# Mixer 0 of a two-layer hybrid decoder trunk: input rows and state parameters on two DMA queues, clearings and both input projection halves placed ahead of the state blocks

## The chip, the cores and the metric

The kernel runs on one core of one Trainium2 chip. The metric is the device time of one execution in microseconds (us), the median of three runs. The engines are named as the profile names them: PE (TensorE, matmul and transpose), DVE (VectorE), ACT (ScalarE), POOL (GpSimd), and SP (SyncE, which only issues DMAs here). A q behind an engine's name (SPq) is its queue of DMA issues.

## What is computed

A trunk of two layers over 256 tokens of width 1024. Each layer adds a token mixer and a channel mixer to the residual stream; only the mixer of layer 0 matters for this change.

```
for l in range(2):
    hn = rmsnorm(x, norm_mix[l])
    x = x + hybrid_mixer(hn, ...)       # mLSTM heads + S5 state-space groups
    hn = rmsnorm(x, norm_ffn[l])
    x = x + (swiglu if l == 0 else moe_swiglu)(hn, ...)
return rmsnorm(x, norm_final)

def hybrid_mixer(h, w_in, ...):
    q, k, v, o, i, f, u = split(h @ w_in)       # u: 512 channels for S5
    ...mLSTM on q, k, v, o with gates i, f...
    # S5, for each of 32 groups g with 64 states p and 16 channels:
    dt = exp(log_dt); ab = exp((a_re + i a_im) * dt)
    bb = (ab - 1) / (a_re + i a_im) * (b_re + i b_im)
    x_t = ab * x_(t-1) + bb @ u_t
    y_t = Re(c @ x_t) + d * u_t
```

## The kernel before, in words

The program is written by hand for each engine: five blocks (SP, POOL, ACT, DVE, PE), each one list of instructions in a fixed order, joined by semaphores. An engine runs its list strictly in order, so an instruction that waits holds everything behind it on that engine.

**Weights.** Weights of 2 MB arrive in a ring of five slots; SP issues their DMAs in the order of `chunk_plan`: u, q, k, v, o of `w_in`, then glu, out and so on. Chunk u (the 512 columns that feed the S5 part) is issued at L802, the other ones at L866, each when the slot's last user has run.

**The start.** SP issues the residual stream x (L800), chunk u (L802), then 17 small DMAs: 12 of parameter rows (L812), 2 of the state matrices' a (L814), log_dt (L816) and 2 gate biases (L818). All 17 count on one semaphore, `s_par`. Then `layer_params(0)` issues b_re and b_im (L823, `b_raw`) and c_re and c_im (L826, `c_raw`), and the gate columns `w_if` (L834). PE's first instruction (L2136) turns the rows into columns (`vec`), and waits for all 17. DVE takes the norm of x (L1296 to L1307), then copies `vec` and `s5p` (L1590 to L1595). PE transposes the normed x (L1956), DVE and ACT copy it out as `hnT` (L1315, L1037).

**The state blocks.** DVE's `prep_factors` (L1323 to L1361, some 38 small operations) works out the discretised factors. `prep_blocks` (L1363 to L1386) clears `blocks` (L1367), multiplies b by the factors into it (L1371 to L1378), copies c into `c_dup` (L1383) and clears `cT` (L1386). PE transposes 4 blocks of b (16 transposes, L1923) and 2 of c (8, L1931); ACT copies b's out (L1025) and DVE c's (`prep_c`, L1396). `turned_c` (L1406 to L1411) makes the c matrices of the even steps and gives `c_ready`, for which only PE's `y` products wait.

**The mixer's order.** On PE (`mixer`, function `channels` at L1969): half 0 of u, the 24 transposes, the gate projection `if` (L2027), the state inputs `bu` of couples 0 and 1 (L1993), half 1 of u, the kernel within a couple `k0` (L1943), and then eight steps, the first of which are: qk 0, bu 2; qk 1, bu 3; y 0 (L2010), qk 2, bu 4; qk 3, bu 5; y 1, v 0, bu 6. A qk is 32 matmuls at L1969. On DVE: `turned_c`, and then for each of eight couples of state pairs one scan block (`s5_couple`, L1422 to L1442, from here on a couple); behind couple 1 the copies of the gates (`gate_start`, L1485 to L1489), behind couple 2 the running sums of the gates (`gate_sums`, L1496 to L1503) and the convolutions (L1472, L1474). On ACT: a copy of each projection (L1085 for u, L1111 for qk), each followed by the sines of one couple (`trig_pair`, L1048 to L1066); behind qk 1 the exp and log of the gates (L1130, L1131), for which `gate_sums` waits. On POOL: the phases of each couple (L957 to L967), and once the decays (L974).

**Banks.** `products()` lists all products in PE's order with the engine that drains each and its PSUM bank; a product waits until the one before it in its bank is drained. The functions `lo` and `hi` hand out banks 0 to 3 and 4 to 7 in turn.

**After the mixer** come the dense SwiGLU, mixer 1 (in the same order, without the state blocks, which `prep_blocks(1)` makes at the end of mixer 0), and the routed SwiGLU, whose weights stream through `m_ring`. Every weight DMA of these stages is released by a product or a copy of the stages before it.

## Time and profile before

| | |
|---|---|
| Median of 3 runs | 1480.25 us (1479.22 to 1481.89) |
| The profiled execution's own time | 1480.46 us |
| Its span in the profile | 1478.4 us |
| PE busy | 1346.0 us (91%) |
| DVE busy | 467.6 us (32%) |
| ACT busy | 278.6 us (19%) |
| POOL busy | 98.0 us (7%) |
| DMA | 423.50 MB, mean 286 GB/s |

The profile is of one execution. Its span runs from the first to the last event of the core; 2.06 us of the execution lie around it. Times in the rows count from the span's start. A timeline merges neighbouring instructions of one line and shape; in its brackets stands how long the engine was idle before, and what ended that wait. Matmul times overlap at their ends, so the distance from one start to the next is what an instruction takes of PE.

### The profile page before, as it was taken

To read this page: it belongs to the slowest core of one execution; us is meant where nothing else is said; L and a number is where in the kernel's file an instruction comes from. 1 tells how busy PE (TensorE), PEld (TensorE's weight loads), DVE (VectorE), ACT (ScalarE), POOL (GpSimd) and SP (SyncE) were. 2 spreads that over 40 slices of the span, in tenths; PEclk is the share of its full clock that TensorE was granted. 3 is DMA by queue.
4 is the path that set the end of the run, shared out by engine and by line. 5 is a ranking of instruction groups with operands and counts; after the bars stand their busy time and mean duration, and the time that the engine had idled before them with its cause. 6 is when DMAs were issued, how large, how long until landed. Compare 5 with 4: busy or idle time off the path is not lost.

```text
span 1478.4 us, 18652 instructions
## 1 busy us (share of the span) xinstructions
PE 1346.0 (91%) x7760; PEld 761.4 (52%) x7760; DVE 467.6 (32%) x1049; ACT 278.6 (19%) x511; POOL 98.0 (7%) x115
## 2 busy tenths in 40 slices
PE   3998879999798886999999999999999999987775
PEld 2765469999785544545445444444433343332321
DVE  6787785555559734022010010101011110100002
ACT  2272234444236200000010100101101001100001
POOL 4240000000343000000000000000000000000000
PEclk9999989999999997999999999999999999999999
DMA  9243055544421208789999959898999999999994
GB/s 283 78 132 132 36 186 207 178 163 150 172 79 65 100 30 354 257 344 409 413 413 411 414 210 418 336 411 337 416 410 412 413 410 414 412 411 416 410 413 203
DMA packets 126734, 423.50 MB, mean 286 GB/s; under 512 B 21632, under 2 KB 23864, under 8 KB 118456
## 3 DMA queue, kind: packets, MB, share of 16 engines
q1 hardware_dynamic: 126648, 422.27, 73.4%
q8 instruction: 64, 1.05, 0.3%
q14 instruction: 22, 0.18, 0.0%
HBM read 421.20 MB, written 1.05 MB: 286 GB/s over the span
## 4 chain that ended last, share of the span: by engine, by line
PE 71%; DMA 14%; DVE 9%; ACT 2%; SPq 2%; issue 2%; POOL 0%; DVEq 0%; ACTq 0%
PE psall L2251 13%; DMA m_ring<-in_moe_w_down_dram 12%; PE psall L2342 11%; PE psall L2265 7%; PE psall L2280 6%; PE psall L1969 3%; PE psall L2353 3%; PE psall L2182 3%; PE psall L2184 3%; PE psall L2183 3%; PE psall L2129 2%; PE psall L2062 2%; PE psall L2228 2%; PE psall L2315 2%; PE psall L2381 2%
## 5 line engine op out<-in xcount | busy, mean ns | idle before, releaser
L2265 PE MATMUL psall<-m_ring,xeT 128*64 128x448 f32 x1024 | 204.2, 547 | 23.0 <-DMA m_ring<-in_moe_w_up_dram 23.0
L2342 PE MATMUL psall<-m_ring,hidT 128*64 128x512 f32 (+1 forms) x672 | 201.0, 597 | 16.0 <-DMA m_ring<-in_moe_w_down_dram 15.1
L2251 PE MATMUL psall<-m_ring,xeT 128*128 128x448 f32 x512 | 195.7, 543 | 0.8 <-DVE xeT L1834 0.8
L2265 PEld LDWEIGHTS psall<-m_ring,xeT 128*64 128x64 f32 x1024 | 74.0, 137 | 141.1 <-issue 139.9
L2251 PEld LDWEIGHTS psall<-m_ring,xeT 128*128 128x128 f32 x512 | 97.3, 191 | 94.1 <-issue 92.9
L2342 PEld LDWEIGHTS psall<-m_ring,hidT 128*64 128x64 f32 (+1 forms) x672 | 72.8, 154 | 135.0 <-issue 119.3
L1856 DVE TENSOR_TENSOR hid<-e_silu,psall 64x448 f32<-64x448 f32 x32 | 19.9, 623 | 354.7 <-ACT e_silu L1216 352.8
L2280 PE MATMUL psall<-m_ring,xeT 128*32 128x448 f32 x1024 | 102.0, 542 | 0.0
L1559 DVE TENSOR_TENSOR w_lo<-ring,w_hi 128x1024 fp32r<-128x1024 f32 x66 | 80.5, 1225 | 68.0 <-ACT w_hi L1171 68.0
L2182 PE MATMUL psall<-hnT_hi,w_hi 128*128 128x256 f32 x352 | 99.6, 283 | 1.2 <-DVE hnT_lo L1692 1.2
L2184 PE MATMUL psall<-hnT_hi,w_lo 128*128 128x256 f32 x352 | 99.5, 283 | 0.0
L2183 PE MATMUL psall<-hnT_lo,w_hi 128*128 128x256 f32 x352 | 98.9, 281 | 0.0
L1969 PE MATMUL psall<-hnT,ring 128*128 128x256 f32 x384 | 85.7, 382 | 2.4 <-ACT hnT L1037 2.4
L950 POOL TENSOR_TENSOR small<-small,neg_half 128x1 f32<-128x1 f32 (+2 forms) x14 | 13.6, 974 | 1084.3 <-DVE small L1298 970.3
L1852 DVE TENSOR_TENSOR hid<-e_silu,psall 128x448 f32<-128x448 f32 x16 | 9.9, 622 | 227.3 <-PE psall L2251 226.3
L1171 ACT ACTIVATE w_hi<-ring 128x1024 fp32r<-128x1024 f32 x66 | 69.3, 1060 | 63.5 <-PE psall L2184 35.9
L1969 PEld LDWEIGHTS psall<-hnT,ring 128*128 128x128 f32 x384 | 72.1, 190 | 13.7 <-issue 3.5
L1230 ACT ACTIVATE hidT<-psall 128x224 f32<-128x224 f32 (+5 forms) x48 | 22.3, 481 | 265.4 <-PE psall L2315 265.2
L2182 PEld LDWEIGHTS psall<-hnT_hi,w_hi 128*128 128x128 f32 x352 | 66.6, 189 | 2.1 <-issue 1.4
L2183 PEld LDWEIGHTS psall<-hnT_lo,w_hi 128*128 128x128 f32 x352 | 66.6, 189 | 0.8
L2184 PEld LDWEIGHTS psall<-hnT_hi,w_lo 128*128 128x128 f32 x352 | 66.3, 188 | 0.0
L2280 PEld LDWEIGHTS psall<-m_ring,xeT 128*32 128x32 f32 x1024 | 30.4, 109 | 63.6 <-issue 63.0
(326 smaller groups left out, 1475.2 us busy)
## 6 DMA issues: line engine op xcount, KB each, us to landing
m_ring<-in_moe_w_gate_dram SPq DMA_DIRECT2D x128, 896.0 KB, 20.0
m_ring<-in_moe_w_up_dram SPq DMA_DIRECT2D x128, 896.0 KB, 17.1
m_ring<-in_moe_w_down_dram SPq DMA_DIRECT2D x64, 1792.0 KB, 19.0
ring<-in_w_in_dram SPq DMA_DIRECT2D x10, 2048.0 KB, 12.9
ring<-in_ffn_w_gate_dram SPq DMA_DIRECT2D x5, 2048.0 KB, 10.4
ring<-in_ffn_w_up_dram SPq DMA_DIRECT2D x5, 2048.0 KB, 7.8
ring<-in_ffn_w_down_dram SPq DMA_DIRECT2D x5, 2048.0 KB, 7.9
ring<-in_w_out_dram SPq DMA_DIRECT2D x4, 2048.0 KB, 8.3
```

The source lines that it names most:

```text
L1171: nc.scalar.activation(ffn_split(n, w_hi), ffn_raw(n), ACT.Copy).then_inc(ffn_hi, 1)
L1559: V.tensor_tensor(ffn_split(n, w_lo), ffn_raw(n), ffn_split(n, w_hi).bitcast(F32), ALU.subtract).then_inc(ffn_lo, 1)
L1969: ins = M(bank(name)[:, i * SEQ:(i + 1) * SEQ], w[:, k, a:a + P], hnT[:, k, :], start=(k == 0), stop=(k == KT - 1))
L2062: ins = M(bank(n)[:, :], hnT[:, k, n[2] * P:(n[2] + 1) * P], v3(chunk((n[0], l)), KT)[:, k, :], start=(k == 0), stop=(k == KT - 1))
L2182: M(y, hi[:, k, :], hnT_hi[:, k, :], start=(k == 0), stop=False)
L2183: M(y, hi[:, k, :], hnT_lo[:, k, :], start=False, stop=False)
L2184: ins = M(y, lo[:, k, :], hnT_hi[:, k, :], start=False, stop=(k == KT - 1))
L2251: ins = M(m_bank(key)[:, 0:MH], x[:, i, 0:P], weights(kind, i, s), start=(i == 0), stop=(i == KT - 1))
L2265: ins = M(m_bank(key)[64 * n:64 * n + 64, 0:MH], x[:, i, 0:64], weights(kind, i, s), start=(i == 0), stop=(i == KT - 1))
L2280: ins = M(m_bank(key)[q:q + 32, 0:MH], x[:, i, base:base + 32], weights(kind, i, s), start=(i == 0), stop=(i == KT - 1))
L2342: ins = M(y, hidT[:, r, 0:shape[0]], rows(r, 512 * n, 512), **ends)
L2353: ins = M(ps[7][32 * q:32 * q + 32, cols:cols + 256], hidT[:, r, base:base + 32], rows(r, 256 * q, 256), **ends)
```

## The change

It does five things.

1. On SP, the 17 small DMAs are issued ahead of chunk u. The four DMAs of b and c of layer 0 go to ACT's queue, as the first instructions of ACT (`state_params(act, 0)`); those of layer 1 stay on SP.
2. The clearings of `blocks` and `cT` are a function of their own, `prep_zeros`. For layer 0 it is the first thing that DVE does; for layer 1 it stands right ahead of `prep_blocks(1)`.
3. In mixer 0, PE runs both halves of u and then `if` ahead of the transposes of the state blocks. ACT copies half 1 of u before the b blocks.
4. In mixer 0, DVE runs `turned_c` behind couple 1 instead of ahead of couple 0.
5. The banks of the front are written out. Behind it, some products of both layers get another bank of 4 to 7: the first head products (`mu` of heads 0 and 1) of mixer 0 now stand behind o 0 and y 2 in their banks, where they stood behind y 3 and o 1.

```diff
--- before.py
+++ after.py
@@ -391,15 +391,21 @@
 
     for l in range(DEPTH):
         norm(l, 0)
-        hi(("u", l, 0), "A")
+        out.append((("u", l, 0), "A", 4))
         if l == 0:
-            prep(0)
-        hi(("if", l), "I")
+            out.append((("u", l, 1), "A", 5))
+        out.append((("if", l), "I", 7))
+        if l == 0:
+            for n in B_BLOCKS:
+                lo((n, l), "A")
+            out.append((("c_re", l), "V", 4))
+            out.append((("c_im", l), "V", 5))
         bu(l, 0)
         bu(l, 1)
-        hi(("u", l, 1), "A")
         if l == 0:
-            hi(("k0", l), "A")
+            out.append((("k0", l), "A", 6))
+        else:
+            out.append((("u", l, 1), "A", 5))
         for q, steps in enumerate(mixer_steps(l)):
             for n in steps:
                 if n[0] == "y":
@@ -792,14 +798,19 @@
         def v3(ap, k):
             return ap.rearrange("p (k n) -> p k n", k=k)
 
+        def state_params(eng, l):
+
+            for i, b in enumerate((s5_b_re, s5_b_im)):
+                eng.dma_start(b_raw[:, i, :, :], b[l].rearrange("(g h) s c -> (h s) g c", h=2)).then_inc(s_bc, 16)
+            for i, c in enumerate((s5_c_re, s5_c_im)):
+                eng.dma_start(c_raw[:, i, :, :], c[l].rearrange("(k g) c s -> (g c) k s", k=CT)).then_inc(s_bc, 16)
+
         block = ctx.enter_context(nc.Block())
 
 
         @block.sync
         def _(sp):
             sp.dma_start(x_res[:, :, :], x.rearrange("b (t p) d -> p (b t) d", p=P)).then_inc(s_x, 16)
-            u_cols = w_in[0, :, U0:U0 + DS5].rearrange("(k p) n -> p k n", p=P)
-            sp.dma_start(v3(ring[:, 0, :], KT), u_cols).then_inc(ring_full[0], 16)
             rows = {"norm_mix": norm_mix, "norm_mlstm": norm_mlstm, "s5_d": s5_d, "norm_s5": norm_s5,
                     "norm_ffn": norm_ffn}
             for l in range(DEPTH):
@@ -818,14 +829,12 @@
                 sp.dma_start(b_if[:, :, i], b.rearrange("l h -> h l"),
                              allow_slow_non_contiguous=True).then_inc(s_par, 16)
 
+            u_cols = w_in[0, :, U0:U0 + DS5].rearrange("(k p) n -> p k n", p=P)
+            sp.dma_start(v3(ring[:, 0, :], KT), u_cols).then_inc(ring_full[0], 16)
+
             def layer_params(l):
-                for i, b in enumerate((s5_b_re, s5_b_im)):
-                    sp.dma_start(b_raw[:, i, :, :],
-                                 b[l].rearrange("(g h) s c -> (h s) g c", h=2)).then_inc(s_bc, 16)
-                for i, c in enumerate((s5_c_re, s5_c_im)):
-                    sp.dma_start(c_raw[:, i, :, :],
-                                 c[l].rearrange("(k g) c s -> (g c) k s", k=CT)).then_inc(s_bc, 16)
                 if l:
+                    state_params(sp, l)
                     wait_drained(sp, ("if", l - 1))
                 else:
                     sp.wait_ge(w_if_zero, 1)
@@ -1093,9 +1102,11 @@
                 trig_pair(l, 0)
                 channels_out(l, 0)
                 if l == 0:
+                    channels_out(l, 1)
                     prep_blocks(0)
                 trig_pair(l, 1)
-                channels_out(l, 1)
+                if l:
+                    channels_out(l, 1)
                 if l == 0:
                     prep_k0(0)
                 for q, steps in enumerate(mixer_steps(l)):
@@ -1170,6 +1181,7 @@
                         act.wait_ge(ffn_used, sum(c[0] != "fu" for c in f_parts[:n - SPLIT + 1]))
                 nc.scalar.activation(ffn_split(n, w_hi), ffn_raw(n), ACT.Copy).then_inc(ffn_hi, 1)
 
+            state_params(act, 0)
             for l in range(DEPTH):
                 if l:
                     turns(l, 0)
@@ -1360,11 +1372,15 @@
                 link(V.tensor_tensor(F(16), F(13), F(17), ALU.mult))
                 link(V.tensor_tensor(F(16), F(11), F(16), ALU.add))
 
+            def prep_zeros(l):
+
+                V.memset(blocks[l], 0.0)
+                link(V.memset(cT[:, 0:2, :, :], 0.0))
+
             def prep_blocks(l):
 
                 F = lambda i: fac[:, i, :]
                 dve.wait_ge(s_bc, 64 * (l + 1))
-                V.memset(blocks[l], 0.0)
                 for s, (a, b) in enumerate(((19, 16), (17, 18))):
                     f_re = F(a).unsqueeze(2).to_broadcast([P, PAIRS, GP])
                     f_im = F(b).unsqueeze(2).to_broadcast([P, PAIRS, GP])
@@ -1383,7 +1399,6 @@
                     ins = V.tensor_copy(c_dup[:, :, :, g, :].rearrange("p a b c -> p (a b) c"),
                                         c_raw[:, :, :, :].rearrange("p a b c -> p (a b) c"))
                 ins.then_inc(blk_ready, 1)
-                link(V.memset(cT[:, 0:2, :, :], 0.0))
 
             def prep_c(l):
                 for i, n in enumerate(("c_re", "c_im")):
@@ -1582,6 +1597,7 @@
                                        in1=xs, op0=ALU.mult, op1=ALU.add).then_inc(drained["V"], 1)
 
 
+            prep_zeros(0)
             dve.wait_ge(s_x, 16)
             for t in range(NT):
                 norm_sum(t, hn[:, t, :])
@@ -1603,10 +1619,13 @@
                     prep_factors(0)
                     prep_blocks(0)
                     prep_c(0)
-                turned_c(l)
+                if l:
+                    turned_c(l)
                 for q in range(COUPLES):
                     s5_couple(l, q)
                     if q == 1:
+                        if l == 0:
+                            turned_c(l)
                         gate_start(l)
                     if q == 2:
                         gate_sums(l)
@@ -1670,6 +1689,7 @@
                 out_s5(l, 1, 0)
                 out_s5(l, 1, 1)
                 if l == 0:
+                    prep_zeros(1)
                     prep_blocks(1)
                 for t in range(NT):
                     for c in range(2):
@@ -1979,7 +1999,7 @@
 
                 channel_pair(0)
                 if l == 0:
-                    prep(0)
+                    channel_pair(1)
 
                 def bu(q):
                     c = q // CPC
@@ -2027,13 +2047,16 @@
                     ins = M(bank(n)[0:F_ROW + NH, 0:SEQ], w_if[:, k, :], hnT[:, k, :],
                             start=(k == 0), stop=(k == KT - 1))
                 done(ins)
+                if l == 0:
+                    prep(0)
                 wait_drained(pe, ("u", l, 0))
                 wait_drained(pe, ("b1_im", l))
                 bu(0)
                 bu(1)
-                channel_pair(1)
                 if l == 0:
                     within(0)
+                else:
+                    channel_pair(1)
                 for q, steps in enumerate(mixer_steps(l)):
                     if q + 2 == 2 * CPC:
                         wait_drained(pe, ("u", l, 1))
```

On PE, from its first transposes to the first qk product. Before (L1956: transposes of the normed x; L1969: u and qk; L1923 and L1931: the state blocks; L2027: `if`; L1943: `k0`):

```order
L1956 MATMUL psall<-ident,hn 128x128 x16
L1969 MATMUL psall<-hnT,ring 128x256 x16
L1923 MATMUL psall<-ident,arena 128x128 x16
L1931 MATMUL psall<-ident,arena 128x128 x8
L2027 MATMUL psall<-hnT,w_if 36x256 x8
L1993 MATMUL psall<-arena 128x128 x2
L1993 MATMUL psall<-arena,bT 128x128 x2
```

And in the changed kernel:

```order
L1976 MATMUL psall<-ident,hn 128x128 x16
L1989 MATMUL psall<-hnT,ring 128x256 x32
L2047 MATMUL psall<-hnT,w_if 36x256 x8
L1943 MATMUL psall<-ident,arena 128x128 x16
L1951 MATMUL psall<-ident,arena 128x128 x8
L2013 MATMUL psall<-arena 128x128 x2
L2013 MATMUL psall<-arena,bT 128x128 x2
```

The second half of u and `if` now stand between the first half and the 24 transposes; nothing of the projections is left between the state inputs and `k0`. (One row of matmuls of the program is two on PE: 16 rows of L1969 are 32 matmuls in the trace.)

On DVE, from the copies of c to the gates. Before (L1386: clearing of `cT`; L1396: `prep_c`; L1406 to L1411: `turned_c`; L1422: a couple's first instruction):

```order
L1383 COPY arena<-c_raw 128x8x64 x2
L1386 MEMSET cT 128x1024
L1396 TENSOR_SCALAR cT<-psall 64x16x16 x4
L1406 TENSOR_TENSOR cT<-cT,fac 128x512
L1407 TENSOR_TENSOR arena<-cT,fac 128x512
L1408 TENSOR_TENSOR arena<-cT,fac 128x512
L1409 TENSOR_TENSOR arena<-cT,fac 128x512
L1410 TENSOR_TENSOR cT<-cT,arena 128x512
L1411 TENSOR_TENSOR arena<-arena 128x512
L1422 TENSOR_TENSOR arena<-psall,arena 128x512
```

In the changed kernel, the same place, and then the end of couple 1:

```order
L1399 COPY arena<-c_raw 128x8x64 x2
L1411 TENSOR_SCALAR cT<-psall 64x16x16 x4
L1437 TENSOR_TENSOR arena<-psall,arena 128x512
L1438 TENSOR_TENSOR arena<-psall,arena 128x512
...
L1457 TENSOR_TENSOR hn<-arena 128x256
L1421 TENSOR_TENSOR cT<-cT,fac 128x512
L1422 TENSOR_TENSOR arena<-cT,fac 128x512
L1423 TENSOR_TENSOR arena<-cT,fac 128x512
L1424 TENSOR_TENSOR arena<-cT,fac 128x512
L1425 TENSOR_TENSOR cT<-cT,arena 128x512
L1426 TENSOR_TENSOR arena<-arena 128x512
L1500 COPY arena<-psall 4x256
```

The couples start right behind `prep_c` (L1411), and the six operations of `turned_c` stand between couple 1 and the copies of the gates.

On ACT, the start of the changed kernel, where before the table load stood first:

```order
L804 DMA b_raw<-in_s_b_re_dram 128x16x16
L804 DMA b_raw<-in_s_b_im_dram 128x16x16
L806 DMA c_raw<-in_s_c_re_dram 128x4x64
L806 DMA c_raw<-in_s_c_im_dram 128x4x64
L1046 ACT_TABLE_LOAD
```

ACT issues the four DMAs before its first table load; on SP their four issues are gone from between the gate biases and `w_if`.

## Rows read from the trace of the kernel before

**Rows 1.** Timeline of PE: start us, us, engine line op, count, [idle before <-releaser].
```profile
14.39 0.43 PE L2136 MATMUL psall<-ident,arena 120*128 120x120 f32 x1 [14.39 <-DMA b_if<-in_b_fgate_dram]
...
15.29 3.65 PE L1956 MATMUL psall<-ident,hn 128*128 128x128 f32 x16 [0.31 <-DVE vec L1593]
20.07 7.14 PE L1969 MATMUL psall<-hnT,ring 128*128 128x256 f32 x32 [1.13 <-ACT hnT L1037]
39.43 3.68 PE L1923 MATMUL psall<-ident,arena 128*128 128x128 f32 x16 [12.21 <-DVE arena L1378]
...
44.04 3.64 PE L2027 MATMUL psall<-hnT,w_if 128*36 128x256 f32 x16
...
49.26 7.17 PE L1969 MATMUL psall<-hnT,ring 128*128 128x256 f32 x32
...
57.22 7.14 PE L1969 MATMUL psall<-hnT,ring 128*128 128x256 f32 x32
...
65.38 7.17 PE L1969 MATMUL psall<-hnT,ring 128*128 128x256 f32 x32
```

**Rows 2.** Windows: stretch, us, busy PE, PEld, DVE, ACT, POOL, PEclk, DMA share, GB/s.
```profile
30.00:32.00 2.00, 0.00 (x0) 0.00 (x0) 2.00 (x2) 1.56 (x5) 1.93 (x2) 0.50 1.06 389
...
700.00:1478.00 778.00, 725.22 (x4218) 312.25 (x4210) 72.20 (x133) 72.19 (x144) 1.96 (x2) 0.99 0.96 386
```

**Rows 3.** Timeline of DVE, from the norm of x to couple 1.
```profile
8.95 1.58 DVE L1307 TENSOR_SCALAR hn<-x_res,small 128x1024 f32<-128x1024 f32 x2 [0.25 <-POOL small L950]
...
27.76 1.76 DVE L1367 MEMSET arena<- 128x2048 f32 x1 [0.49 <-DVE fac L1361]
...
43.78 1.75 DVE L1396 TENSOR_SCALAR cT<-psall 64x256 f32<-64x256 f32 x4 [2.54 <-PE psall L1931]
45.56 0.69 DVE L1406 TENSOR_TENSOR cT<-cT,fac 128x512 f32<-128x512 f32 x1
...
50.55 0.69 DVE L1422 TENSOR_TENSOR arena<-psall,arena 128x512 f32<-128x512 f32 x1
...
55.99 0.69 DVE L1422 TENSOR_TENSOR arena<-psall,arena 128x512 f32<-128x512 f32 x1
```

**Rows 4.** Timeline of ACT: the copy of qk 1, and the gates' table load.
```profile
72.59 0.60 ACT L1111 ACTIVATE arena<-psall 128x512 f32<-128x512 f32 x1 [4.83 <-PE psall L1969]
...
75.98 1.28 ACT L1130 ACT_TABLE_LOAD   x1
```

**Rows 5.** Timeline of DVE, from the end of the gates' copies to the heads.
```profile
62.66 0.41 DVE L1489 SCALAR_TENSOR_TENSOR arena<-arena 4x256 f32<-4x256 f32 x1
67.79 0.69 DVE L1422 TENSOR_TENSOR arena<-psall,arena 128x512 f32<-128x512 f32 x1 [4.72 <-ACT arena L1066]
...
73.57 0.42 DVE L1442 TENSOR_TENSOR hn<-arena 128x256 f32<-128x256 f32 x1
79.45 0.41 DVE L1496 SCALAR_TENSOR_TENSOR arena<-arena 4x256 f32<-4x256 f32 x1 [5.46 <-ACT arena L1131]
...
134.44 0.48 DVE L1515 SCALAR_TENSOR_TENSOR arena<-psall,small,cmask 128x256 f32<-128x256 f32 x1 [0.45 <-PE psall L2072]
```

**Rows 6.** Timeline of SP's queue: start and length of each issue.
```profile
1.28 0.46 SPq L802 DMA_DIRECT2D ring<-in_w_in_dram  x1
...
7.94 0.30 SPq L818 DMA_DIRECT2D b_if<-in_b_fgate_dram  x1
```

**Rows 7.** DMA issues of 0 to 16 us: KB each, median us from issue to landing.
```profile
ring<-in_w_in_dram SPq DMA_DIRECT2D x1, 2048.0 KB, 10.2
x_res<-in_x_dram SPq DMA_DIRECT2D x1, 1024.0 KB, 5.1
...
c_raw<-in_s_c_im_dram SPq DMA_DIRECT2D x1, 128.0 KB, 2.6
```

**Rows 8.** Tile b_raw in 60 to 200 us: layer 1's two loads, issue to landing.
```profile
DMA to landing us min/median/max: 4.0/4.2/4.5
```

**Rows 9.** Timeline of PE: 4 transposes of layer 1's blocks.
```profile
187.73 0.63 PE L1923 MATMUL psall<-ident,arena 128*128 128x128 f32 x4
```

## The prediction

> **What bounds the kernel now.** I read the windows first. From 700 us to the end the DMA engines are 96% busy at 386 GB/s and PE 93% [rows 2]: the routed weights stream there. Every weight DMA of that stage is released by an event of the stages before it, so the stage keeps its length and starts when mixer 1 lets it. I take what the front gains to reach the end one for one.
>
> The timeline of PE then shows the front. PE's first instruction waits until 14.39 us for the last small row, its transposes of x start at 15.29, and the first half of u at 20.07. Then it stands still for 12.21 us until DVE has made the state blocks at 39.43, though the second half of u (49.26) and `if` (44.04), which need nothing of DVE, stand behind the blocks [rows 1]. In the hole the granted clock falls to 0.50 [rows 2], 1.2 of 2.4 GHz.
>
> The reader should also see who pays for the late second half. DVE has its first couple at 50.55 [rows 3], but waits 4.72 us ahead of couple 2 and 5.46 us ahead of `gate_sums` at 79.45, both for ACT [rows 5], and ACT had waited 4.83 us for PE's qk 1 [rows 4]. So PE's place in its list sets DVE's `gate_sums`. From there to the heads DVE has hardly a gap; the gain is thus counted at `gate_sums`.
>
> **The change, part by part, on the clock of the profiled execution.**
>
> *Projections ahead of the blocks.* Without any earlier start, PE runs two halves of u (7.14 each) from 20.07 to 34.35, and `if` (3.6, from 44.04 to about 47.6) to 37.9 [rows 1]. DVE's blocks, before at 39.43, lose the clearing of 1.76 us [rows 3] and are there at 37.7. PE and the blocks meet; the hole of 12.21 us is gone. With no hole PE stays at the full clock. The 24 transposes took 4.61 at the half clock (39.43 to 44.04 [rows 1]); four of layer 1's took 0.63 [rows 9], so 24 take 3.8, to 41.7. I take this, and 4.6 as the other bound. `prep_c` (43.78 to 45.56, 1.8 [rows 3]) then ends at 43.5, and the couples can start, since `turned_c` no longer stands ahead of them.
>
> *The clearings.* Both lie on DVE ahead of x, where it is idle (its norm ends at 10.53 [rows 3], it has nothing before x lands, 5.1 us after its issue [rows 7]). They need some 2.7 us (1.76, and half of it for half as many elements); if DVE were late there, up to 2 us would come back. The clearing of `cT` was free before too: it lay inside DVE's wait of 2.54 us for PE [rows 3]. In layer 1 they only change places on DVE: 0.
>
> *DVE's way to `gate_sums`.* A couple took 5.44 (50.55 to 55.99 [rows 3]) with POOL idle for most of it, and 6.2 (67.79 to 73.99 [rows 5]) beside POOL's phases. Now phases lie beside nearly every couple; for couples 0 and 1 I take 5.8 each: 43.5 to 55.1. `turned_c` takes 5.0 (45.56 to 50.55 [rows 3]): 60.1. The gates' copies 1.7 (from couple 1's end, 55.99 + 5.44 = 61.4, to 63.1 [rows 3, 5]): 61.8. Couple 2, 6.2: 68.0.
>
> *PE's and ACT's way to `gate_sums`.* PE does `bu` 0 and 1 (1.7) and `k0` (0.8, up to 57.22 [rows 1]) by 44.3, where `k0` waits for `prep_c`. A qk with its `bu` is 8.16 (57.22 to 65.38 [rows 1]): qk 0 by 52.5, qk 1 by 59.6. ACT needs 3.4 to copy and make the sines (72.59 to 75.98 [rows 4]) and 3.5 for exp and log (to 79.45 [rows 5]): 66.5.
>
> So `gate_sums` stands at 68.0 by DVE and 66.5 by ACT, before at 79.45: **11.4 to 12.9 earlier**. I take 11.8, near the DVE end. The new wait, that y 0 needs `turned_c` (60.1), costs nothing: PE comes to y 0 only behind qk 1 and `bu` 3, at 60.7. Behind y 0 PE has qk 2, which nobody on DVE wants before its second convolution.
>
> *Rows ahead of chunk u.* The last row is issued at 7.94 [rows 6] and lands at 14.39 [rows 1], 6.4 us later, since 3 MB of x and u lie ahead of it in SP's queue; behind no such load a small DMA lands in 2.6 [rows 7]. Now only x is ahead: issued at about 7.5, landed at about 10.3. Then the norm of x becomes the last to come: it ends at 10.53 [rows 3]. The gain has 14.3 less 10.5, or 3.8, as its upper end. The lower end is 0, as b and c now go out beside x. In layer 1 a load of b took 4.0 to 4.5 to land [rows 8], 2 more than a small one, all in short packets. If a share of this falls on x, the norm ends at 11.6. I take **2.6**, nearer to the upper end, because the 3 MB become 1 MB.
>
> The Trainium skill speaks against this part ("DMA: Bandwidth & Descriptors", section "Issuing engines are not separate DMA queues"): DMAs of all issuing engines run on the same 16 DMA engines and interleave, and a second issuer only saves issue time. By that rule the second queue gains nothing for the rows; the b and c packets are mixed with x's, and the sum would move from 1465.6 toward rival B's. No row of before shows two queues at once, so I can't say yet whether the trace agrees.
>
> *Chunk u.* It was issued at 1.28 [rows 6] and landed 10.2 later [rows 7], at 11.5. Now it is issued at about 7.9. By the same 10.2 it lands at 18.1; x (5.1) took half of that, so 13 to 18.1. It is wanted at 20.07 less 2.6, 17.5. I charge nothing; the bound is 0.6, more if b and c hold it up. The chunks q to o follow it; 2 MB at 389 GB/s [rows 2] are 5.4 us, so q is there by 24 and o by 40, and qk 0 begins at 41. ACT's four issues lie ahead of 17 us, where it had nothing to do.
>
> *Banks.* The head's first product no longer waits for y 3's drain: DVE's wait of 0.45 at 134.44 [rows 5] goes. I take **0.4**.
>
> **The sum:** 11.8 + 2.6 + 0.4 = 14.8 us of 1480.46, or **1465.6 us**. The profiled execution lies 0.2 above the median, which I leave aside.
>
> **The rivals.** A measurement can tell 0.2% (3 us) here.
>
> *A. As above.* Bounds: 10.4 (old price of the transposes, DVE's upper durations) to 12.9 for the first part, 0.5 to 3.8 for the second, 0 to 0.9 for the banks. Likely ends: 17.6 and 11, so 1462.9 to 1469.5. Chance 0.70.
>
> *B. The short packets go first.* ACT's b loads (two of 4.0 to 4.5 us [rows 8]) start with x on the same engines and hold it or the rows for all of 3.8 us. For: nothing orders the two queues. Against: their bytes are a quarter of x's. Then only 11.8 + 0.4 is gained: 1468.3. By the skill's rule on interleaving, named above, this case has its ground. Chance 0.13.
>
> *C. Chunk u comes late.* It is the last of 18 issues now, and b and c push it. If it lands at 22, 4.5 after it is wanted, PE and all behind it lose that: 14.8 less 4.5, 1470.2. For: 18.1 by its old landing is already late by 0.6. Against: once it runs, its 2 MB need 5.4 us. Chance 0.10.
>
> *D. The gain does not arrive.* Should the stream of routed weights be paced by something that the front does not move, the time stays at 1480. Against: all its DMAs wait for products of the core. Chance 0.04.
>
> *E. Slower: rows held behind ACT's descriptors.* If SP's 17 issues were each held up, as ACT's b and c are generated at the same time, `s_par` comes late, and with it everything. Each us of it costs one us; it decides from 14.8 us on: rows complete later than at 14.4 + 12.2 = 26.6, instead of 10.3. That takes 17 issues of 1.3 us instead of the 0.38 each that they take now (1.74 to 8.24 on SP [rows 6]). At 30 us the time is 1484. For: a large load on a full queue does block its issuer. Against: rows are few and short. Chance 0.03.
>
> **How the numbers follow.** The forecast is A's, 1465.6. The range 1462.5 to 1470 holds nearly all of A, B, and about half of C: 0.84 of the cases; it is cut no closer, as A's ends are bounds of single terms and not sharp. Faster by over 0.2% are A, B, C: 0.93. Within 0.2%: D, 0.04. Slower: E, 0.03.
>
> **What would show it.** In the new profile: rows complete by 10 to 12 us, transposes of x from 12.7 instead of 15.29; PE busy without a hole from u's first half to the blocks and granted clock 1.0 from 26 to 44 us; the first couple's start near 41; `gate_sums` near 65 instead of 79.45; everything from there, the routed stream too, some 14 us earlier at equal length. Wrong would be: a wait for the ring's DMA ahead of the first half of u (C); x's norm later than 12 (B); a wait ahead of y 0 for `turned_c`; a routed stage that starts earlier and ends at the same time (D).

## The result, and the profile after

| | runs | median, us | range | ratio to before, 95% |
|---|---|---|---|---|
| before, beside the first | 4 | 1480.74 | 1479.22 to 1481.89 | |
| the change | 4 | 1472.62 | 1470.17 to 1473.38 | 0.9943 [0.9926, 0.9960] |
| before, in a later session | 9 | 1480.10 | 1478.81 to 1482.52 | |
| the change again (e13) | 5 | 1469.21 | 1468.99 to 1471.05 | 0.9930 [0.9916, 0.9943] |

The change gains 8.1 us, against 14.8 forecast, and 1472.62 lies outside the range of 1462.5 to 1470. Repeated in another session it gains 10.9, and 1469.21 lies just inside. The profiled execution, the longest of the first four, took 1473.38 us, with a span of 1471.3, 7.1 under that of before. PE is busy for 1351.3 us (92%), DVE for 469.5, ACT for 277.3; DMA still moves 423.50 MB.

The timeline of PE after the change, read against [rows 1] (columns as there):

```profile
11.04 0.43 PE L2159 MATMUL psall<-ident,arena 120*128 120x120 f32 x1 [11.04 <-DMA b_if<-in_b_fgate_dram]
...
11.94 3.65 PE L1976 MATMUL psall<-ident,hn 128*128 128x128 f32 x16 [0.31 <-DVE vec L1609]
16.72 14.05 PE L1989 MATMUL psall<-hnT,ring 128*128 128x256 f32 x64 [1.13 <-ACT hnT L1046]
30.70 3.64 PE L2047 MATMUL psall<-hnT,w_if 128*36 128x256 f32 x16
34.27 1.97 PE L1943 MATMUL psall<-ident,arena 128*128 128x128 f32 x16
...
39.57 7.17 PE L1989 MATMUL psall<-hnT,ring 128*128 128x256 f32 x32
...
78.08 0.65 PE L2030 MATMUL psall<-arena 32*32 32x128 f32 x8 [3.67 <-DVE hn L1457]
...
80.52 8.82 PE L2085 MATMUL psall<-ring,hnT 128*128 128x512 f32 x16
```

The rows arrive 3.35 us earlier (11.04, before 14.39), both halves of u run in one piece from 16.72, and the blocks start at 34.27 instead of 39.43 with no hole ahead of them. But there is a new hole: 3.67 us ahead of y 1, on DVE, and behind it v 0 takes 8.82 us. In the kernel before PE stood 0.88 us there, and v 0 took 7.13:

```profile
92.27 0.42 PE L2010 MATMUL psall<-arena 32*32 32x128 f32 x8 [0.88 <-DVE hn L1442]
...
93.63 7.13 PE L2062 MATMUL psall<-ring,hnT 128*128 128x512 f32 x16
```

DVE's timeline, read against [rows 3, 5]:

```profile
9.15 1.58 DVE L1319 TENSOR_SCALAR hn<-x_res,small 128x1024 f32<-128x1024 f32 x2 [0.25 <-POOL small L959]
...
36.72 1.75 DVE L1411 TENSOR_SCALAR cT<-psall 64x256 f32<-64x256 f32 x4 [1.93 <-PE psall L1951]
...
38.49 0.69 DVE L1437 TENSOR_TENSOR arena<-psall,arena 128x512 f32<-128x512 f32 x1
...
64.25 0.41 DVE L1511 SCALAR_TENSOR_TENSOR arena<-arena 4x256 f32<-4x256 f32 x1
...
96.29 0.43 DVE L1476 SCALAR_TENSOR_TENSOR arena<-arena 128x256 f32<-128x256 f32 x1 [4.22 <-ACT arena L1085]
```

Couple 0 is 12.06 us earlier, and `gate_sums` 15.2 (64.25, before 79.45), a little more than was counted. Then, at 96.29, DVE stands 4.22 us for ACT, where before the same wait was 0.66:

```profile
108.26 0.43 DVE L1461 SCALAR_TENSOR_TENSOR arena<-arena 128x256 f32<-128x256 f32 x1 [0.66 <-ACT arena L1076]
```

In the changed kernel ACT had been waiting itself:

```profile
89.38 0.60 ACT L1127 ACTIVATE arena<-psall 128x512 f32<-128x512 f32 x1 [4.68 <-PE psall L2085]
```

The windows show PE's clock. First the changed kernel: the full front, y 1 and v 0, the first output products, mixer 1's first products, the routed stream (us, busy PE, PEclk, DMA share, GB/s).

```profile
20.00:60.00 40.00, 39.42 (x332) 1.00 0.71 236
78.00:90.00 12.00, 11.92 (x68) 0.75 0.21 81
140.00:154.00 14.00, 12.57 (x40) 0.62 0.00 0
392.00:404.00 12.00, 10.77 (x39) 0.75 0.00 0
700.00:1471.00 771.00, 716.73 (x4170) 0.99 0.96 386
```

The same three middle places in the kernel before:

```profile
92.00:104.00 12.00, 11.73 (x77) 1.00 0.46 170
151.00:165.00 14.00, 12.26 (x45) 0.88 0.01 3
400.00:412.00 12.00, 10.76 (x50) 0.93 0.00 0
```

The front runs at the full clock (PEclk 1.00 is 2.4 GHz, 0.50 is 1.2), as forecast, but in three places behind idle stretches the granted clock is 0.75, 0.62 and 0.75, where it was 1.00, 0.88 and 0.93. The routed stream has its old shape [rows 2].

**Where the 15.2 us went.** The table has the start of the same instruction in profiled executions, as us earlier than in the kernel before. e1 to e15 are the kernels of the next section. hmT are the eight transposes between the output products of mixer 0, and Y 0 is y 0 of mixer 1.

| | before, us | change | e13, again | e1 | e2 | e3 | e4 | e6 | e9 | e11 | e15 |
|---|---|---|---|---|---|---|---|---|---|---|---|
| blocks' transposes | 39.43 | 5.2 | 5.3 | 3.3 | 1.8 | 5.4 | 5.0 | 2.9 | 0.2 | 5.5 | 1.7 |
| `gate_sums` | 79.45 | 15.2 | 15.3 | 3.4 | 11.8 | 15.4 | 15.0 | 12.9 | 0.6 | 15.5 | 11.7 |
| y 2 | 114.26 | 12.0 | 12.5 | 3.4 | 8.7 | 12.5 | 8.1 | 12.3 | 0.6 | 12.8 | 11.0 |
| first output product | 152.05 | 11.1 | 11.8 | 3.4 | 7.8 | 12.1 | 13.8 | 14.6 | 0.9 | 12.9 | 10.2 |
| hmT | 171.50 | 7.8 | 11.4 | 3.4 | 4.5 | 11.8 | 13.8 | 16.4 | 2.7 | 14.7 | 9.7 |
| x transposes, mixer 1 | 397.76 | 9.3 | 11.4 | 3.4 | 6.0 | 11.7 | 13.7 | 18.0 | 2.8 | 14.5 | 9.7 |
| Y 0, mixer 1 | 438.26 | 6.0 | 10.4 | 3.4 | 2.7 | 10.7 | 12.7 | 18.7 | 4.5 | 15.2 | 8.7 |
| routed stage | 581.68 | 7.2 | 11.5 | 3.4 | 3.9 | 8.7 | 13.8 | 22.6 | 7.8 | 18.6 | 9.8 |
| span | 1478.4 | 7.1 | 11.5 | 3.2 | 3.8 | 9.1 | 14.2 | 22.1 | 9.7 | 20.1 | 10.1 |

So the front's gain was whole at `gate_sums` and was lost in steps: 3.2 us by y 2, 0.9 to the output products, 3.3 in the output products, 3.3 at the start of mixer 1; 1.5 came back ahead of the dense SwiGLU and 1.1 behind Y 0 of mixer 1. From the routed stage on nothing changes, as the forecast had it.

### The profile page after: what moved, and what is told of

It is laid out like the page before. It is cut to its first block, busy times and chain, and to the rows that moved or that the text cites. A ratio compares the mean times of both kernels' runs of the same rounds, so it can differ in the third digit from the quotient of the medians.

```text
span 1471.3 us, 18652 instructions
## 1 busy us (share of the span) xinstructions
PE 1351.3 (92%) x7760; PEld 764.5 (52%) x7760; DVE 469.5 (32%) x1049; ACT 277.3 (19%) x511; POOL 96.0 (7%) x115
## 2 busy tenths in 40 slices
DMA packets 126734, 423.50 MB, mean 288 GB/s; under 512 B 21632, under 2 KB 23864, under 8 KB 118456
## 4 chain that ended last, share of the span: by engine, by line
PE 73%; DMA 13%; DVE 9%; ACT 2%; issue 2%; SPq 1%; POOL 0%; DVEq 0%; ACTq 0%
PE psall L2274 13%; DMA m_ring<-in_moe_w_down_dram 12%; PE psall L2365 11%; PE psall L2288 8%; PE psall L2303 6%; PE psall L2376 3%; PE psall L1989 3%; PE psall L2205 3%; PE psall L2207 3%; PE psall L2206 3%; PE psall L2152 3%; PE psall L2085 3%; PE psall L2251 2%; PE psall L2338 2%; PE psall L2404 2%
## 5 line engine op out<-in xcount | busy, mean ns | idle before, releaser
L2365 PE MATMUL psall<-m_ring,hidT 128*64 128x512 f32 (+1 forms) x672 | 201.0, 597 | 17.2 <-DMA m_ring<-in_moe_w_down_dram 16.4
L2152 PE MATMUL psall<-ring,hn 128*128 128x512 f32 x128 | 62.1, 646 | 2.5 <-ACT hn L1169 2.5
## 6 DMA issues: line engine op xcount, KB each, us to landing
m_ring<-in_moe_w_up_dram SPq DMA_DIRECT2D x128, 896.0 KB, 17.1
```

The lines of the kernel that those rows point to most:

```text
L2152: ins = M(bank(n)[:, :], mixT[:, k0 + k, t * P:(t + 1) * P], v3(chunk(("out", l, c)), KT)[:, k0 + k, :], start=(k == 0), stop=(k == 3))
L2365: ins = M(y, hidT[:, r, 0:shape[0]], rows(r, 512 * n, 512), **ends)
```

## The experiments

Two theories. **T1**: the front's gain is real, but PE now runs ahead of DVE; where it then stands, its granted clock falls, and the products behind run at half speed. **T2**: a fixed chain of DVE and ACT absorbs the gain, and the clock is a symptom.

### e1 and e2: the two parts apart

e1 is the kernel before with only the two queues: u's issue moved behind the small rows, b and c of layer 0 on ACT's queue.

```diff
-            sp.dma_start(v3(ring[:, 0, :], KT), u_cols).then_inc(ring_full[0], 16)
...
+            sp.dma_start(v3(ring[:, 0, :], KT), u_cols).then_inc(ring_full[0], 16)
...
+            state_params(act, 0)
```

> The kernel before with part 1 of the change alone (17 rows ahead of chunk u, b and c on ACT's queue). In the changed kernel x's first transposes came 3.35 us earlier (15.29 to 11.94). Theory 1 (what the front gains is real, and PE's granted clock gives part of it back later, by where holes of PE fall): the first transposes are 3.35 earlier, gate_sums near 76.1 instead of 79.45, and the end is 3.35 earlier give or take 2 us by the clock: 1475 to 1479. Theory 2 (from gate_sums on a fixed chain of DVE and ACT absorbs what comes earlier): gate_sums near 76.1, the end within 1 us of before. Theory 3 (the early DMAs disturb later loads): gate_sums later than 76.1.

Measured: 1477.2 us, ratio 0.9981 [0.9971, 0.9991]. The shift of 3.4 stands in every row of the table, to the end.

e2 is the changed kernel without this part, so it has the clearings and the order alone.

> The changed kernel with part 1 undone (chunk u second, then the rows, b and c on SP). Theory 1: gate_sums at 64.25 + 3.35 = 67.6, the hole of PE ahead of y 1 as in the changed kernel (3.7 us), its end some 3 us later than the changed kernel's: 1474 to 1478, with the clock's spread. Theory 2: gate_sums at 67.6 and the end equal to the changed kernel's 1472.6. Sum of the two halves (this one and rows only) against before: theory 1 the same as the whole change's 8.1 within 3 us.

Measured: 1474.28, 0.9953 [0.9939, 0.9966]. 11.8 us at `gate_sums`, 3.8 in the span. The parts add up at `gate_sums` (3.4 + 11.8 = 15.2) and in the profiled spans (3.2 + 3.8 = 7.0, measured 7.1). The part that shifts PE and DVE alike keeps its gain. The part that moves PE against DVE does not: in its profiled execution, the longest of five, two thirds of the 11.8 are lost, by the median, 6.4 us under the kernel before, nearly half. Nothing at the end of the kernel absorbs a gain, which ends rival D.

### e3: idle products in the hole ahead of y 1

The added matmuls, fillers from here on, compute nothing that is used.

```diff
+            def warm(name, n):
+                for _ in range(n):
+                    M(bank(name)[:, 0:SEQ], ident[:, :], cmask[:, :], start=True, stop=True)
...
+                    if (l, c) == (0, 1):
+                        warm(n, 14)
                     pe.wait_ge(tile_done, l * COUPLES + CPC * (c + 1))
```

> The changed kernel; ahead of y 1 in mixer 0, PE fills its hole of 3.67 us with 14 matmuls of 128x256 on constants (some 3.1 us), whose result the product overwrites. Theory 1 (clock): the granted clock stays 1.00 in y 1 and v 0, v 0 takes 7.1 instead of 8.8 and y 1 1.4 instead of 2.4; ACT's copy of v 0 is 2.7 us earlier, DVE's wait ahead of gelu_outer(0) falls from 4.22 to about 1.5, y 2 is 2 to 2.7 us earlier (99.6 to 100.3 instead of 102.28). End 0 to 3 us earlier than the changed kernel. Theory 2 (fixed chain): the same wait of 4.2 and y 2 at 102.3.

Measured: 1471.53, 0.9944 [0.9931, 0.9958]. PE's timeline:

```profile
74.12 6.31 PE L1940 MATMUL psall<-cmask,ident 128*128 128x256 f32 x28
...
81.72 7.13 PE L2091 MATMUL psall<-ring,hnT 128*128 128x512 f32 x16
```

v 0 takes 7.13 us instead of 8.82, but 14 fillers (28 matmuls in the trace) take 6.31, more than the hole, and v 0 starts 1.2 later. The two cancel, so y 2 moves by 0.5 us only. Too large a dose: inconclusive for y 1, done again as e15.

### e4 and e7: useful work in the hole

e4 is the changed kernel with v 0 ahead of y 1 and o 0 ahead of y 2 on PE, in both layers; e7 has the same edit on the kernel before.

```diff
-    return [[("qk", l, 0)], [("qk", l, 1)], [("y", l, 0), ("qk", l, 2)], [("qk", l, 3)], [("y", l, 1), ("v", l, 0)],
-            [("v", l, 1), ("tr", l)], [("y", l, 2), ("o", l, 0)], [("o", l, 1)]]
+    return [[("qk", l, 0)], [("qk", l, 1)], [("y", l, 0), ("qk", l, 2)], [("qk", l, 3)], [("v", l, 0), ("y", l, 1)],
+            [("v", l, 1), ("tr", l)], [("o", l, 0), ("y", l, 2)], [("o", l, 1)]]
```

> The changed kernel with v 0 ahead of y 1 and o 0 ahead of y 2 in both mixers: the holes ahead of y 1 (3.67 us) and y 2 (3.16) are filled with useful products. Theory 1: no hole ahead of y 1, v 0 at the full clock and done near 81.5 instead of 89.3, DVE has no wait ahead of gelu_outer(0) and (1) (4.22 and 2.47 in the changed kernel), and DVE's couples alone set the end of the scans: the last couple ends about 6 us earlier. End 4 to 8 us earlier than the changed kernel in all, both mixers together: 1465 to 1469. Theory 2: DVE's waits go as well, but the tail starts no earlier than y 3, so 1470 to 1473.

> The kernel before, with v 0 ahead of y 1 and o 0 ahead of y 2 on PE, the order that gave 1467.9 on top of the change. It asks whether this order is worth 5 us by itself, or only since the change made PE arrive early. T1: in the kernel before PE stands 0.88 us ahead of y 1, so v 0 delays y 1 by 6 us and with it the outer steps of DVE; gain at y 2 to o 0 at most 3.2 us, loss at y 1; 1477 to 1484. T2 or an order that is better whatever the front does: 1474 to 1476, 5 us less than before.

Measured: e4 1467.91, 0.9921 [0.9906, 0.9936]; e7 1479.52, 1.0000 [0.9989, 1.0011]. On the kernel before the order is worth nothing. On the changed kernel its profiled execution (1466.34, among the two shortest of five) keeps 13.8 us at hmT and 14.2 in the span:

```profile
74.50 7.13 PE L2085 MATMUL psall<-ring,hnT 128*128 128x512 f32 x16
81.56 0.42 PE L2030 MATMUL psall<-arena 32*32 32x128 f32 x8
```

y 1 goes later by 3.5 us and y 2 by 3.8 against the change, yet y 3 comes 4.3 earlier (116.11, changed kernel 120.36): ACT gets v 0 early and does not stand at 89.38 any more. By the trace, then, the changed front wants another order behind it. The times are weaker: e4's interval overlaps that of the repeat (1469.21, [0.9916, 0.9943]), so they alone don't show a gain of the order.

### e9 and e11: the same fillers on both kernels

Both have 6 idle products ahead of head 2's numerator, 3 ahead of head 3's, and 12 ahead of mixer 1's first transposes; e9 on the kernel before, e11 on the changed one.

```diff
+                if (l, what) == (1, 0):
+                    open_bank(pe, ("xT", l, what, 0))
+                    warm(("xT", l, what, 0), 12)
                 pe.wait_ge(hn_ready, (2 * l + what + 1) * NT)
...
                         open_bank(pe, n)
+                        if h >= 2:
+                            warm(n, 6 if h == 2 else 3)
                         wait_drained(pe, ("sc", l, h))
```

> The kernel before with the idle products ahead of head 2 and 3 in both layers and ahead of mixer 1's first transposes, as a control for what the fillers are worth without the change. T1: in the profiled execution of before the clock there was mostly 1.0 already, so little: 1478 to 1480. If the fillers bring 3 us or more here as well, then the half clock behind these holes is a cost of both kernels and not what the change lost.

> The changed kernel with exactly the idle products of e9 (ahead of heads 2 and 3 in both layers, ahead of mixer 1's first transposes), none ahead of y 1 and y 2. Against e9 (1473.4) it prices the change where these three places are at the full clock in both kernels. T1 (the change's gain was lost at the half clock behind idle stretches, in layer 0's y 1 as well as here): about 3 us of the loss (v 0 and y 1) stay, and the rest arrives: 1459 to 1462, a change worth 11 to 14 us. T2 (the loss lies in a chain of DVE and ACT): the change stays worth the 8 us that it was without fillers, 1465.

Measured: e9 1473.40, 0.9954 [0.9942, 0.9966]; e11 1461.83, 0.9885 [0.9869, 0.9901]. T1's 1459 to 1462 for e11 was met, and its 1478 to 1480 for e9 missed: the fillers give 7.4 us in the kernel before too, and 7.4 in the changed one (e13, 1469.21, is of e11's session). So most of the half clock there is a cost of both kernels, not a loss of the change. What it does is spread: with the same program, the output products lost 3.3 us of the shift in the first profile and 0.4 in e13. e11's windows at the output products and at mixer 1's start:

```profile
139.00:153.00 14.00, 14.00 (x55) 1.00 0.00 1
385.00:397.00 12.00, 10.76 (x50) 1.00 0.01 1
```

With the clock held at these places in both, the change is worth 1473.40 less 1461.83, or 11.6 us. Each against the kernel before of its own session makes it 10.9, the two profiled spans 10.4. That leaves 3.6 to 4.8 us of the 15.2, which no clock at these places explains.

### e15: the right dose at y 1

e3 with 8 fillers instead of 14.

> The changed kernel with 8 idle products (3.6 us) ahead of y 1 of layer 0 alone, where PE stands 3.67 us; e3 had 14 there (6.3 us), which delayed y 1 by 2.3 us and so couldn't show what the clock alone costs. T1: y 1 near 78, 1.4 us long, v 0 7.1 us instead of 8.8, y 2 near 99.5 and a shift there of 15 us instead of 12.0 to 12.5; the time 2 to 3 us below 1469 to 1472. T2 (DVE and ACT absorb it): PE at the full clock, y 2 at 101.5 to 102.

Measured: 1470.14, 0.9929 [0.9914, 0.9944].

```profile
77.80 3.72 PE L1940 MATMUL psall<-cmask,ident 128*128 128x256 f32 x16
81.45 0.42 PE L2036 MATMUL psall<-arena 32*32 32x128 f32 x8
...
82.81 7.13 PE L2091 MATMUL psall<-ring,hnT 128*128 128x512 f32 x16
...
103.26 0.65 PE L2036 MATMUL psall<-arena 32*32 32x128 f32 x8 [3.15 <-DVE hn L1457]
```

And DVE's, at the instruction that waited 4.22 us in the changed kernel:

```profile
97.27 0.43 DVE L1476 SCALAR_TENSOR_TENSOR arena<-arena 128x256 f32<-128x256 f32 x1 [0.66 <-ACT arena L1085]
```

Of the numbers expected, y 1 near 78 and y 2 at 99.5 were missed, since this execution's front was 3.5 us slower (`gate_sums` at 67.72, below). Read as a loss between `gate_sums` and y 2, which the front doesn't enter, T1 holds: without fillers the shift falls by 3.2, 2.8, 3.1, 3.0, 2.7 and 3.1 us (the change, e13, e2, e10, e11, e14), with 8 fillers by 0.7 (e15) and 0.6 (e6). So the clock behind this hole costs 2.0 to 2.6 us there. v 0 takes 7.13 us with fillers and 8.4 to 8.8 without, and from 81 to 93 us the granted clock is 1.00. The chain of T2 exists, but it hands on what PE does: ACT copies v 0 (89.38 above) ahead of the sines and of what DVE waits for at 96.29, and with the fillers DVE's wait is 0.66, as in the kernel before. The time expected, 1466 to 1470, was missed by a little, and the time itself doesn't tell e15 from the changed kernel. In the time such fillers show only where the later holes are filled too (e6, below).

### e14: a shared bank in mixer 1

```diff
         else:
-            out.append((("u", l, 1), "A", 5))
+            out.append((("u", l, 1), "A", 4 + (turn["hi"] + 1) % 2))
```

> The changed kernel, with u 1 of layer 1 in PSUM bank 4 instead of 5 and nothing else. In both traces of the changed kernel PE stands 0.78 us ahead of qk 0 of mixer 1, waiting for ACT's copy of u 1 (in the kernel before it ran through), since both products now have bank 5; from u 1's start to Y 0 mixer 1 takes 36.6 us in every changed kernel at the full clock, 35.6 in the kernel before. If the shared bank is the cause: no wait ahead of qk 0, 35.6 us again, and the end 1.0 us earlier, near 1468.3 (a difference that the timing alone can hardly show, the trace can). If not: 36.6 as before.

Measured: 1470.63, 0.9930 [0.9917, 0.9942]. PE in mixer 1, first e13, then e14:

```profile
403.59 7.17 PE L1989 MATMUL psall<-hnT,ring 128*128 128x256 f32 x32
411.54 4.77 PE L1989 MATMUL psall<-hnT,ring 128*128 128x256 f32 x21 [0.78 <-ACT arena L1094]
```

```profile
406.15 14.08 PE L1989 MATMUL psall<-hnT,ring 128*128 128x256 f32 x64
```

The wait is gone, and from u's start to Y 0 mixer 1 takes 35.60 us, as in the kernel before (35.59); e13 took 36.61. The change costs 1.0 us there, by giving u 1 of layer 1 the bank that qk 0 has next. But it does not reach the end. From Y 0 to the routed stage the changed kernel and e13 take 142.2 us, e14 143.4, as the kernel before (143.4): what e14 wins ahead of Y 0 it lacks behind it. Why the stretch behind Y 0 is shorter with the shared bank stays open. Nor does the median show a gain.

### e10: `turned_c` back ahead of couple 0

```diff
-                if l:
-                    turned_c(l)
+                turned_c(l)
                 for q in range(COUPLES):
...
-                        if l == 0:
-                            turned_c(l)
                         gate_start(l)
```

> The changed kernel with one part undone: the turned C blocks of layer 0 are made ahead of couple 0 again and not behind couple 1. My sum counted DVE's 5.0 us of it as only moved (it lies ahead of gate_sums in both places), with couple 0 five us later and y 0 nearer. T1: gate_sums within 0.5 us of the changed kernel's 64.24; PE has to wait for couples 0 to 1, and the time stays within 3 us of 1472.6. Rival (this order is a separate gain): gate_sums and the end 4 to 5 us later, 1477.

Measured: 1471.50, 0.9937 [0.9923, 0.9951]. `gate_sums` stood at 66.14, 1.9 us later, but so did the blocks already (36.15, changed kernel 34.27). Behind the blocks it costs nothing; `turned_c` is only moved, as counted. One small thing is different: PE has no idle time ahead of y 0 here. In the changed kernel `turned_c` ends at 56.38 us, and y 0 starts 0.2 behind it:

```profile
56.59 0.42 PE L2030 MATMUL psall<-arena 32*32 32x128 f32 x8 [0.56 <-issue]
```

### e13: the change once more

> The changed kernel once more, without any edit, for its interval and for a second profiled execution. T1: where the clock falls differs from one execution to the next, so the shift at hmT (7.8 us) and at mixer 1's Y 0 (6.0 us) may differ by 1 to 4 us while that at y 2 (12.0) stays; the shift at gate_sums stays at 15.2. T2: all shifts repeat within 0.5 us.

Measured: 1469.21, 0.9930 [0.9916, 0.9943]. `gate_sums` (15.3) and y 2 (12.5) repeat within 0.5 us; hmT is 11.4 instead of 7.8 and Y 0 10.4 instead of 6.0:

```profile
78.00:90.00 12.00, 12.00 (x73) 0.79 0.21 80
139.00:153.00 14.00, 12.57 (x44) 0.80 0.00 0
390.00:402.00 12.00, 10.76 (x51) 0.99 0.00 0
```

One part of the loss, y 1 and v 0 (0.79, the change 0.75), is there in both. The others, 2.9 of the 3.3 us in the output products and 2.3 of the 3.3 in mixer 1, come and go with the execution.

### e6, e8, e12, e16, e17: toward a better version

e6 is e11 with 8 fillers ahead of y 1 and 6 ahead of y 2 in layer 0; e8 is e4 with e11's. e12 adds to e8 6 fillers ahead of `bu` of couple 3 and 3 ahead of y 2 in layer 0, 8 ahead of the router's transposes and 5 ahead of its positions:

```diff
+                elif (l, what) == (1, 1):
+                    open_bank(pe, ("xT", l, what, 0))
+                    warm(("xT", l, what, 0), 8)
...
+                                    if (l, i) == (0, 6):
+                                        warm(n, 6)
...
+                    if l == 0 and c == 2:
+                        warm(n, 3)
...
+            open_bank(pe, ("pos",))
+            warm(("pos",), 5)
             pe.wait_ge(route_mask, 1)
-            open_bank(pe, ("pos",))
```

e16 is e12 with e14's bank, and e17 is e16 with this:

```diff
+                if l == 0:
+                    open_bank(pe, ("u", l, 0))
+                    warm(("u", l, 0), 3)
                 have_hnT(l, 0)
                 chunk_wait(pe, ("u", l))
```

> The changed kernel with idle products (identity by mask, 256 columns, about 0.45 us each at the full clock) put in front of PE's waits: 8 ahead of y 1 and 6 ahead of y 2 of layer 0 (the idle times there are 3.67 and 3.16 us), 6 ahead of the numerator of head 2 and 3 ahead of head 3's in both layers (2.95 and 1.43 us), 12 ahead of the first transposes of mixer 1 (6.99 us). They compute nothing that is used. Theory T1 (the idle time lowers the granted clock, and the products behind it run at half speed): y 1 takes 1.4 us instead of 2.4, v 0 7.1 instead of 8.8, the shift against the kernel before stays near 12 us at hmT (7.8 without fillers) and near 11 at mixer 1's Y 0 (6.0 without), and the time is 1467 to 1469. Theory T2 (a chain of DVE and ACT absorbs it, the clock is a symptom): PE shows the full clock, but y 2 and hmT stand where they stood, 1471 to 1474.

> The changed kernel with both: v 0 ahead of y 1 and o 0 ahead of y 2, and the idle products ahead of head 2 and 3 and of mixer 1's first transposes. T1: the half clock behind the remaining holes goes, z and the output products and mixer 1's u run at full speed: another 1 to 3 us below the 1467.9 of the order alone, 1465 to 1467. T2: 1468.

> A candidate for the best version: v 0 ahead of y 1 and o 0 ahead of y 2 in both layers, the idle products of e8, and more of them ahead of bu of couple 3 (6) and y 2 (3) in layer 0, ahead of the transposes for the router (8) and ahead of its positions (5). T1: 1 to 3 us below the 1456.3 and 1459.0 of the two earlier versions, 1454 to 1457. If the fillers fill up a place where PE is itself the bound, it is slower than those, 1458 to 1461.

> e12 (1454.4) with u 1 of layer 1 in bank 4. As for e14: 1 us, 1453.4, or nothing.

> e16 with 3 idle products between the transposes of x and u in layer 0, where PE stands 1.1 to 1.8 us. In five profiled executions so far u's 64 products took 14.05 us and the blocks' transposes began at 34.0 to 34.3; in four they took 15.6 to 16.0, with the first 14 of them at half rate, and the blocks' transposes began at 36.2 to 36.5. If that is the clock behind this idle time, the blocks start at 34 to 34.5 here and the median falls by about 1 us, to 1452; if it is something else (chunk u still arriving), u takes 14 to 16 us again.

| | median, us | range | ratio, 95% |
|---|---|---|---|
| e6 | 1456.34 | 1454.62 to 1458.44 | 0.9832 [0.9819, 0.9845] |
| e8 | 1459.01 | 1458.06 to 1460.32 | 0.9857 [0.9843, 0.9872] |
| e12 | 1454.44 | 1451.31 to 1455.95 | 0.9823 [0.9809, 0.9836] |
| e16 | 1453.64 | 1452.82 to 1457.07 | 0.9820 [0.9805, 0.9835] |
| e17 | 1452.16 | 1451.30 to 1453.39 | 0.9807 [0.9795, 0.9820] |

Fillers ahead of y 1 and y 2 of layer 0 are all that e6 has more than e11, and they bring 5.5 us (1461.83 to 1456.34; the intervals of the ratios are apart). The order of e4 in their place (e8) brings 2.8, with intervals that just touch. e6 gained 12 us more than T1 had asked of it, since T1 had priced the half clock by its difference to the kernel before. e17 beats both kernels: 28.4 us under the one before, 17 to 20 under the change. e16's bank can't be told from nothing by the time, nor can e17's fillers from e16.

## Why the prediction was wrong

**What held.** The rows: 3.35 us, counted 2.6. The way to `gate_sums` without them (e2): 11.8, counted 11.8. That it is equal is in part luck. The sum for DVE gave 11.4, and 11.8 was chosen above it; in e2 couple 0 starts at 41.89, 1.6 earlier than the 43.5 counted, and from there to `gate_sums` DVE takes 25.8 us, 1.3 more than counted. The first is the price of the transposes: 24 took 2.9 us (34.27 to 37.13), not 3.8. DVE sets `gate_sums`, and the clock is 1.00 from 20 to 60 us. `turned_c` behind couple 1 costs `gate_sums` nothing (e10), though y 0 does wait for it by some 0.6 us, which the prediction had named as a sign of being wrong; PE has time to spare there, since it stands 3.67 us at y 1. The clearings delay the norm of x by 0.2 us (it ends at 10.73, before 10.53), and the rows come later still (11.04). The stream keeps its length, and whatever reaches it reaches the end (e1). Rivals B and E did not come. The DMA issues of the changed kernel (KB, us to landing):

```profile
x_res<-in_x_dram SPq DMA_DIRECT2D x1, 1024.0 KB, 5.2
b_raw<-in_s_b_re_dram ACTq DMA_DIRECT2D x1, 128.0 KB, 6.7
b_raw<-in_s_b_im_dram ACTq DMA_DIRECT2D x1, 128.0 KB, 7.8
```

x lands 5.2 us after its issue, before 5.1 [rows 7]. b beside it takes 6.7 and 7.8; in the kernel before, behind x and u in SP's queue, the same two loads took 6.0 and 6.8, and layer 1's, later, 4.0 to 4.5 [rows 8]. The Trainium skill says that DMAs of several issuing engines interleave on the same DMA engines ("DMA: Bandwidth & Descriptors", "Issuing engines are not separate DMA queues"). The trace fits that, with b paying and not x. Its further step, that a second issuer saves only issue time, is not refuted by e1's 3.4 us. The rows stood ahead of b and c in SP's queue before too, so the likely cause is that chunk u no longer stands ahead of them; no run has the new order without the second queue.

**The step that failed** is "I take what the front gains to reach the end one for one", with "From there to the heads DVE has hardly a gap". I priced the hole that the change removes and none that it makes. PE gained more than DVE (17.0 us at y 0, 15.2 at `gate_sums`), and the list behind it was written for a late PE. It is ahead of DVE by 3.67 us at y 1, falls to the half clock, and v 0 takes 8.82 us instead of 7.13, at a place where ACT, and through it DVE, now wait for PE. The shift loses 2.7 to 3.2 us between `gate_sums` and y 2 in six kernels without fillers there, and 0.6 to 0.7 in two with them (e15, e6), so 2.0 to 2.6 of it are the clock. By the trace of e4 the order avoids most of it. With the later losses (below), 7.1 and 11.5 of the 15.2 us reach the end in the two profiled executions of the change.

**A second step, of a different kind.** "In layer 1 they only change places" was said of the clearings. I had no term for the projections of layer 1, whose banks the change sets anew: +1.0 us at Y 0 (e14), which comes back behind it. The **banks** term of 0.4 was right at its place and does not last. DVE's wait ahead of the heads is gone, and from y 3 to the first head product PE takes 0.75 us less; by the numerator of head 2 0.2 of that is lost, and 0.7 more in this numerator, which runs at the half clock behind an idle stretch of 2.95 us (with e11's fillers this last loss is 0.03).

**The account**, for the changed kernel as e13 shows it: 15.3 at `gate_sums`, less 2.8 to y 2, less 0.5 in o 0 and o 1 behind y 2's own hole (15.35 us, before 14.80; e6, with fillers there, gains 1.7 instead), plus 0.75 for the banks, less 0.2, less 0.7 in the numerator of head 2. That is 11.8 at the output products. Then 0.4 go in these and 1.0 for the bank of layer 1, and 1.2 come back behind Y 0: 11.5 at the routed stage. These are the rows of one execution, and not a test of the account. Beside it stand 10.9 in the median of e13, and 10.4 to 11.6 for e11 against e9. The first measurement's missing 3 to 4 us lie in the output products and in u of mixer 1, at 0.62 and 0.75 of the clock.

**The range.** Its bounds came from single durations of the front. A term for the clock behind holes that exist in both kernels was missing; in two profiled executions of one program it moves the span by 4.4 us (1471.3 and 1466.9). The sum itself is 1465.7, not 1465.6, which changes nothing.

## What to carry to other kernels

When a front is sped up, follow the engine that gains most to the first place where it is now too early. It stands there, and behind it at the half clock, and what it does then may be what another engine waits for. Look for work that can be put into that place before you count the gain (e4: 13.8 of 15.0 us kept at hmT in its trace, from a change of order that gives 0 without the faster front). And give every fixed buffer that a change assigns a line of its own in the sum, in each layer, then follow it to the end: e14's microsecond is won at Y 0 and gone at the routed stage.

## What was not expected of the hardware

Idle stretches of PE of 2.95 and 1.43 us ahead of heads 2 and 3 of layer 0, the same places of layer 1, and one of 7 us ahead of mixer 1 cost 7.4 us together, in both kernels alike; a few products that compute nothing win them back (e9, e11). The Trainium skill states the mechanism ("TensorE: Matmul & The Clock Gate", Part 1): the clock is halved by default and activity releases it. The trace agrees: in the output products and at mixer 1's start the granted clock is 0.62 and 0.75 in the changed kernel, and 1.00 in both with e11's fillers.

The granted clock of the windows doesn't always tell. In e15 u's 64 products of layer 0 took 17.11 us, in the changed kernel 14.05; the windows name 1.00 for both. First e15's window, then the durations of the 64 products (ns, least, median, most; e15, then the changed kernel):

```profile
17.00:21.00 4.00, 3.88 (x9) 1.00 0.68 166
```

```profile
L1993 PE MATMUL psall<-hnT,ring x64: 379/379/764, 17.1 to 33.9; 128*128 128x256 f32 x64
```

```profile
L1989 PE MATMUL psall<-hnT,ring x64: 378/380/455, 16.7 to 30.4; 128*128 128x256 f32 x64
```

Some of e15's took 764 ns, twice the 379 of the others, and their weight loads up to 337 ns instead of 190. Of 14 profiled executions with both halves of u in a row, nine took 14.05 us, and five (e6, e10, e12, e14, e15) 15.6 to 17.1. With it goes the start of the blocks' transposes, 34.0 to 34.8 or 36.2 to 37.7 (e2, without the earlier rows, left aside), and `gate_sums` by 2 to 3.5 us. PE stands 1.1 to 1.8 us ahead of u in all of them without fillers there. That it is the clock behind this idle time is likely from the 764; e17 with fillers there took 14.05, but so did others without, and one profile doesn't show it. Rival C's ground is near: in most of these executions chunk u's landing ends the wait, at 16.4 to 17.5 us. From the start of x's transposes to u it is 4.78 us where ACT ends the wait (the change), and up to 5.44 (e17) where the chunk does, so it costs up to 0.7.
